# An encoder layer in float32r products: big buffers moved by 32 bytes, four raw weight buffers in the first up product, layer norm in finer pieces, two groups of steps one unit earlier

## The reference

```python
h   = x @ w_in          # recurrent branch, gate, two attentions
y   = concat(rms(rglru(h) * gelu(gate)), rms(band_attention(h)), rms(forgetting_attention(h)))
x   = LN1(alpha * x + y @ w_out)
x   = LN2(alpha * x + relu(x @ w_up) ** 2 @ w_down)
# LN(x) = (x - mean) * rsqrt(var + eps) * g + b
```

## Time and profile before

| | us |
|---|---|
| median of 3 runs (lowest, highest) | 2536.57 (2535.47, 2537.32) |
| the profiled execution | 2535.64 |
| its span, first to last instruction | 2533.7 |
| TensorE busy | 2420.8 |
| VectorE busy | 1291.5 |
| ScalarE busy | 843.5 |

### The profile page before, as it was taken

One profiled execution on the slowest core, in us unless ns is written; L12 is line 12 of the kernel. 1 busy time (PEld: TensorE's weight loads), 2 busy tenths in 40 slices (PEclk: granted clock), 3 DMA queues, 4 the chain that ended last, 5 costly groups with the idle time before them and its releaser, 6 DMA issues.

```text
span 2533.7 us, 41915 instructions
## 1 busy us (share of the span) xinstructions
PE 2420.8 (96%) x17703; PEld 2371.6 (94%) x17703; DVE 1291.5 (51%) x1092; ACT 843.5 (33%) x891; POOL 125.6 (5%) x183
## 2 busy tenths in 40 slices
PE   8999999996996989898999999989999999999997
PEld 7999999995885989898999999989999999999997
DVE  3312555335446577556777777753333333333358
ACT  3222444215333355653444444431212121111132
POOL 2000233100020100000000000000000000000000
PEclk9999999998997999999999999999999999999999
DMA  7222333324441456674555555572323323323244
GB/s 207 83 83 70 104 110 96 102 90 141 127 150 43 150 175 206 203 240 133 170 170 170 170 170 170 170 251 84 120 80 118 112 84 121 122 84 121 84 167 158
DMA packets 310768, 342.43 MB, mean 135 GB/s; under 512 B 11124, under 2 KB 284728, under 8 KB 310088
## 3 DMA queue, kind: packets, MB, share of 16 engines
q1 hardware_dynamic: 271888, 291.95, 36.5%
q10 hardware_dynamic: 35912, 36.49, 4.2%
q0 software_dynamic: 2864, 12.44, 1.5%
HBM read 295.95 MB, written 46.47 MB: 135 GB/s over the span
## 4 chain that ended last, share of the span: by engine, by line
PE 90%; DVE 5%; ACT 2%; issue 2%; DMA 1%; ACTq 0%; DVEq 0%; SPq 0%
PE psum L419 53%; PE psum L1841 29%; PE psum L1949 4%; DVE w_lo L409 1%; PE psum L1795 1%; ACT w_hi L873 1%; PE psum L1709 1%; ACT w_hi L405 0%; PE psum L1750 0%; DVE resid L1118 0%; PE psum L1764 0%; DMA raw<-in_w_up 0%; DVE ln_sumsq L1217 0%; PE psum L1936 0%; PE psum L1653 0%
## 5 line engine op out<-in xcount | busy, mean ns | idle before, releaser
L409 DVE TENSOR_TENSOR w_lo<-raw,w_hi 128x2048 fp32r<-128x2048 f32 x168 | 390.1, 2322 | 493.7 <-ACT w_hi L405 425.1
L405 ACT ACTIVATE w_hi<-raw 128x2048 fp32r<-128x2048 f32 x138 | 264.2, 1915 | 895.7 <-PE psum L419 760.5
L419 PE MATMUL psum<-x_hi,w_hi 128*128 128x288 f32 x1280 | 278.7, 299 | 3.1 <-DVE w_lo L409 3.1
L419 PE MATMUL psum<-x_lo,w_hi 128*128 128x288 f32 x1280 | 275.1, 296 | 0.0
L419 PE MATMUL psum<-x_hi,w_lo 128*128 128x288 f32 x1280 | 275.1, 296 | 0.0
L1841 PE MATMUL psum<-x_b_hi,w_hi 128*128 128x288 f32 x768 | 230.9, 301 | 20.6 <-DVE w_lo L409 11.9
L1430 DVE TENSOR_TENSOR acc<-psum,acc 128x576 f32<-128x576 f32 x96 | 72.7, 757 | 347.3 <-PE psum L419 347.3
L1841 PE MATMUL psum<-x_e_hi,w_hi 128*128 128x288 f32 x768 | 228.2, 297 | 9.8 <-DVE w_lo L1352 9.8
L1841 PE MATMUL psum<-x_b_hi,w_lo 128*128 128x288 f32 x768 | 230.3, 300 | 0.0
L1841 PE MATMUL psum<-x_e_hi,w_lo 128*128 128x288 f32 x768 | 228.7, 298 | 0.0
L419 PE MATMUL psum<-h_hi_even,w_hi 128*128 128x288 f32 x1024 | 220.4, 296 | 6.5 <-DVE h_lo_even L1416 6.5
(11 more groups left out here) (335 smaller groups left out, 4841.6 us busy)
## 6 DMA issues: line engine op xcount, KB each, us to landing
raw<-in_w_down SPq DMA_DIRECT2D x72, 1024.0 KB, 5.3
raw<-in_w_up SPq DMA_DIRECT2D x64, 1024.0 KB, 6.0
raw<-in_w_in SPq DMA_DIRECT2D x40, 1024.0 KB, 5.4
raw<-in_w_out SPq DMA_DIRECT2D x24, 1024.0 KB, 5.3
a_even<-in_w_up SPq DMA_DIRECT2D x24, 1024.0 KB, 6.4
h_scratch<-c_tile ACTq DMA_DIRECT2D x48, 288.0 KB, 2.2
h_even<-h_scratch SPq DMA_DIRECT2D x8, 1152.0 KB, 8.1
h_odd<-h_scratch SPq DMA_DIRECT2D x8, 1152.0 KB, 10.7
```

The costliest lines, as they stand in the source:

```text
L405: act.activation(WH[s][:, :, :], RAW[s][:, :, :], ACT.Copy).then_inc(hi_done, 1)
L409: dve.tensor_tensor(WL[s][:, :, :], RAW[s][:, :, :], WH[s][:, :, :].bitcast(F32), ALU.subtract).then_inc(lo_done, 1)
L419: last_mm = pe.matmul(PS[:, 2 * to + h, 0:c], w, x[:, kk, HALF * h:HALF * h + c], start=(first and n == 0), stop=(final and n == 2))
```

## The change

1. A spare buffer of 32 bytes per partition is put ahead of the large buffers. All of them then start on multiples of 64 bytes. Some small buffers inside (gate weights, `tr`, `a`, `u`, the forget weights) move from multiples of 64 to 32 past one.
2. In 1A, units 0 to 19 use four raw buffers (`RAW`, and two new ones where the lo parts of y rows 8 to 15 lie until w_out is done), units 20 to 31 two.
3. The reductions over 8 tiles are replaced: each square tile is folded by one 128 x 1152 add (`fold`), the two are added (`join`), and TensorE sums the four 288-column pieces with its ones matrix. So `variance` makes 4 float32 matmuls for 2, and `mean(1)` 4 for 2.
4. The layer norm steps are spread: one quarter at a time where two stood together, and for h = 0 the variance is read after unit 11, where it was read in unit 13. F1 and F2 are split one unit earlier. For h = 1, `shifted(1)` and `shifted(3)` go ahead of the snapshot of the next groups. The combinations come two units later.
5. `sigma1` and `sigma2` of the first superblock are made during the last unit of 1A, ahead of its last add.
6. The split of the first chunk of h goes ahead of the last add of phase 1B.

```diff
+N_DEEP = 20
+        sb("align_64_bytes", [128, 8])
...
+            for a in range(2 * N_SB):
+                if a == 2 * N_SB - 2:
...
+                buf, landed, _ = raw_1a(a)
+                if a in (2, 3):
+                    sp.wait_ge(unit_done, N_1A + 2)
+                else:
+                    sp.wait_ge(lo_done, N_1A + a + (1 if a < 2 or a >= N_DEEP + 2 else -1))
+                sp.dma_start(buf[:, :, :], up_unit(0, a % 2, a // 2)).then_inc(landed, 16)
...
+            def hi_1a(a):
+                buf, landed, count = raw_1a(a)
+                act.wait_ge(landed, count)
+                act.wait_ge(unit_done, N_1A + a + 1)
+                act.activation(WH[a % 2][:, :, :], buf[:, :, :], ACT.Copy).then_inc(hi_done, 1)
...
+                elif g in (6, 7):
+                    shifted(2 * (g - 6) + 1, 1)
-                elif g == 8:
+                elif g == 9:
                     act.wait_ge(combo, 1)
                     factor_hi(F5, X1["b00"])
...
+            def fold(T, n, p, h):
+                dve.wait_ge(ln_sq, 2 * h + p + 1)
+                a = T[:, 0:n, :]
+                dve.tensor_tensor(a, a, T[:, n:2 * n, :], ALU.add).then_inc(ln_ss, 1)
+            def join(h):
+                dve.wait_ge(ln_ss, 3 * h + 2)
+                a = SQ[0][:, 0:4, :]
+                dve.tensor_tensor(a, a, SQ[1][:, 0:4, :], ALU.add).then_inc(ln_ss, 1)
...
             for a in range(2 * N_SB):
+                if a == 2 * N_SB - 1:
+                    dve.wait_ge(unit_done, N_1B + 1)
+                    sigma1(0, 0)
+                    sigma2(0, 0)
...
-                for n in range(2):
-                    mm = pe.matmul(PS[:, 5, 0:HALF], ones[:, :], NV[n][:, :], start=(n == 0), stop=(n == 1))
+                for n in range(4):
+                    mm = pe.matmul(PS[:, 5, 0:HALF], ones[:, :], SQ[0][:, n, :], start=(n == 0), stop=(n == 3))
```

More of the change, by code:

```diff
@@ L202, in encoder_step @@
         r = Region()
-        NS = [r.sb(f"ln1_sum{i}", [128, HALF]) for i in range(3)]
-        NV = [r.sb(f"ln1_sumsq{p}", [128, HALF]) for p in range(2)]
+        NS = r.sb("ln1_sum", [128, HALF])
         ND, RS = (r.sb(n, [128, HALF]) for n in ("ln1_sd", "ln1_rstd"))
@@ L208, in encoder_step @@
         F7, F3 = ([r.sb(f"x1_{n}_{p}", [128, UK, HALF], F32R) for p in ("hi", "lo")] for n in ("e7", "b11"))
+        r.close()
+        r = Region()
+        r.sb("y_lo_upper", [128, UK * TOK])
+        RAWX = [r.sb(f"raw_extra{s}", [128, UK, UC]) for s in range(2)]
         r.close()
@@ L269, in encoder_step @@
         raw_in = [sem(f"raw_in{s}") for s in range(2)]
+        rawx_in = [sem(f"raw_extra_in{s}") for s in range(2)]
         hi_done, lo_done = sem("hi_done"), sem("lo_done")
@@ L936, in superblock @@
                 act.dma_start(h_rows(0, g)[:, :, HALF:TOK], CQ[0][:, :, :]).then_inc(c_out[0], 16)
+                if end:
+                    for p in range(4):
+                        h_split(0, 0, p)
                 if not end:
@@ L1352, in lo_1b, with lo_1a @@
                 dve.tensor_tensor(WL[par][:, :, :], src[:, :, :], WH[par][:, :, :].bitcast(F32), ALU.subtract).then_inc(lo_done, 1)
+            def lo_1a(a):
+                buf, _, _ = raw_1a(a)
+                dve.wait_ge(hi_done, N_1A + a + 2)
+                dve.tensor_tensor(WL[a % 2][:, :, :], buf[:, :, :], WH[a % 2][:, :, :].bitcast(F32), ALU.subtract).then_inc(lo_done, 1)
+            for v in range(16):
+                add_out(v, 0)
+                if v == 8:
+                    for m in range(2):
+                        dve.wait_ge(o_ev[m], 8)
+                    centre(0, 0)
+                elif v == 9:
+                    centre(3, 0)
+                elif v == 12:
+                    rstd(0)
+                    scaled(0, 0)
+                elif v == 13:
+                    scaled(3, 0)
+                add_out(v, 1)
+                if v == 8:
+                    centre(1, 0)
+                elif v == 10:
+                    fold(SQ[1], 4, 1, 0)
+                elif v == 12:
+                    scaled(1, 0)
+                n = N_O2 + v + 2
+                if v < 14:
+                    lo(dve, n // 2, n % 2)
+                else:
+                    lo_1a(v - 14)
+                if v == 8:
+                    centre(2, 0)
+                elif v == 9:
+                    fold(SQ[0], 4, 0, 0)
+                elif v == 10:
+                    join(0)
+                elif v == 12:
+                    scaled(2, 0)
+                elif v == 13:
+                    factor_lo(F1, X1["b00"], 1)
+                elif v == 14:
+                    factor_lo(F2, X1["b10"], 2)
@@ L1387, in superblock @@
                     lo(dve, G_D, 0)
+                    for p in range(4):
+                        h_remainder(0, 0, p)
                 dve.wait_ge(unit_done, unit_1b(g, 4) + 3)
@@ L1395, in superblock @@
                     lo(dve, G_D, 1)
-            dve.wait_ge(unit_done, N_1B + 1)
-            sigma1(0, 0)
-            sigma2(0, 0)
             dve.wait_ge(sig, 2)
```

241 lines of the change are left out of this document (106 added, 135 removed).

## The result

| | before | after |
|---|---|---|
| median, us (lowest, highest) | 2536.95 (2535.47, 2539.39) | 2520.16 (2518.71, 2521.33) |
| profiled execution, its span | 2535.64, 2533.7 | 2520.07, 2518.3 |

These medians are of four executions each. The ratio is 0.9933, 95% interval 0.9921 to 0.9946: faster by 0.67%. The forecast was 2520.7. That the number is met does not make every term of the sum right, so the gain is first divided by stage. The starts are those of TensorE's first matmul in each stage, read from the timelines of the two profiled executions.

The account below looks back on a forecast made before the run. TensorE, busy 96% of the span, bounds the kernel, so only its work and waits count. Gains less costs sum to 15.9 us off the profiled 2535.64: 2519.7, plus 0.93 for the median, 2520.7; range 2400 to 2542.

Parts of the forecast that it names:

- I am wrong if the pace moved: Closing test: forecast wrong if the matmul pace moved, or if ScalarE waits for raw buffers anywhere in 1A.
- 32 bytes: Large buffers moved to multiples of 64 bytes: no effect on VectorE, DMA or TensorE, taken as 0.
- Start of 1A: Phase 1A's first matmul: 4.7 us earlier, at about 925.4, wait left 2.7, plus 1.0 for less slow clock.
- Finer norm, units 13 and 14: Norm in 1A: gains 2.1 and 2.7 us at unit 13; costs 2.0 for rows, 2.4 and 1.0 at unit 14.
- Four raw buffers: Raw-buffer loads in 1A: one visible ScalarE wait, costing at most 0.9 us, removed; gain 0.9.
- Sigma: Wait before the first sigma unit: 9.8 us down to 3.0, gain 6.8, plus 1.2 for slow clock.
- h: Wait before the down product, 6.5 us: gain 1.9, VectorE's last add of 1B releasing it instead of the remainder.
- Rival 1: All matmuls reach the better token half's pace or just below: 27 us at most, 20 taken, 2501; chance 0.12.
- Rival 3: Weights and moving operand both on multiples of 64 slow every matmul: 2548 at 1.6 ns each; chance 0.08.
- Rival 2: TensorE's fixed 13.3 ns per matmul shrinks: gain of up to about 11 ns, pace 126 or 122; chance 0.30.
- Rival 4: Moved steps in 1A gain nothing: three places with new or lasting waits eat 14 us, 2535; chance 0.07.
- The half-counted slow stretches: Behind shortened waits, half the 1.2 GHz slow stretch credited: 1.0 at 1A's start, 1.2 at sigma.

Follow-up runs that it names:

- no_pad: The changed kernel without the spare buffer of 32 bytes, all else as changed; 2521.45 us, ratio to before 0.9944.
- again: The changed kernel itself run once more, unaltered; 2520.35 us (2512.26 to 2521.49), ratio to before 0.9925.
- pad_alone: The kernel before with only the 32 spare bytes added; 2533.92 us, ratio to before 0.9989.
- norm_back: The changed kernel with scalings and shifts of h = 1 in pairs again, the adds kept; 2520.56 us, ratio to before 0.9932.
- two_raw: The changed kernel with two raw buffers throughout phase 1A; 2518.36 us, ratio to before 0.9934.
- sigma_back: The changed kernel with the two first sigma sums behind the last add of 1A again; 2525.40 us, ratio to before 0.9957.
- h_back: The changed kernel with the first h chunk's splits and remainders behind all of 1B again; 2523.46 us, ratio to before 0.9944.
- better: The changed kernel with 1B's last add behind the first h remainder and h = 1 shifts one place later; 2507.21 us, ratio to before 0.9877.

## Why the forecast was right, and where only its sum was
The moved steps are best tested by `no_pad`, which has them without the bytes. Its stages against those of before gained 5.4 us (1A starts at 924.72), 7.3 (1A took 227.48), 2.4 (1B took 517.87) and -1.0 (the down product), 14.1 in all, against 4.7, 8.1, 3.1 and 0, 15.9 in all. So the mechanism was right for the steps that carry the gain (the start of 1A, sigma, h), and the sum of all steps was 1.8 us too high, less than the clock alone moves 1A from one execution to the next. That the forecast of the changed kernel came within 0.5 us is in part luck, as the terms below show. By the prediction's own test, "I am wrong if the pace moved", it was wrong on the 32 bytes.

- **Start of 1A**: forecast 925.4, measured 923.24. The chain was right, the wait 3.0 for 2.7. Without the bytes it is 924.72, so 0.7 us of the difference are the steps, and the rest comes with the bytes, by w_in's faster pace (1.5 us here, 3.2 in `again` with 921.56), which the term "32 bytes: 0" did not have. This step, the largest but sigma, was not taken back by itself: its 5.4 us are read from the wait, 8.4 before and 3.0 in `no_pad` and in the changed kernel, 8.6 in `pad_alone`.
- **Finer norm, units 13 and 14**: chain and distance right to 0.1 us (8.86 for 8.8). The two gains and two costs of this part sum to 1.4; `norm_back` measured none that stands out of the clock's scatter. The cost of 2.0 for the added float32 rows was not tested by a run of its own. That the slow stretch "goes, or is swallowed by the next wait" held in one execution and not in the other.
- **Four raw buffers**: 0.9 forecast, 0 measured (`two_raw`). The term was an upper bound ("at most 0.9"), taken as the value. The wait of 4.3 us belonged to the old order.
- **Sigma**: 6.8 forecast, 6.7 in the wait, 6.5 in the start of 1B and 5.1 in the median (`sigma_back`). The 1.2 for the clock did not come in the first pair of profiles: 23 slow matmuls for 21.
- **h**: 1.9 forecast, 2.0 measured in the wait (`h_back`), with the releaser named in advance. The same reasoning showed that only the order of one add was in the way, and `better` took it away.
- **32 bytes**: 0 forecast. This is the term that was mis-sized: a gain of 2.9 us in w_in, a loss of 1.2 to 2.2 in 1B (517.87 us in `no_pad`; 519.05 and 520.07 in two executions of the changed kernel), a loss of about 1.5 in 1A (1536 matmuls by 1.0 ns), and by chance a gain of up to 8 in the down product. The parts nearly cancel, and that is luck: nothing in the prediction said that they would. Rival 1 (all at the better pace) came true as far as some stretches go: 130.0 ns is even below the 131.8 that I had as the better half, and with 96 bytes it is 10 us of gain. Rival 3 (every matmul slower) came true in 1A and 1B of the changed kernel alone, by about 1 ns. The slowest place, 64 spare bytes, 5.8 us above `again`, has the large buffers 32 past a multiple of 64 and the weights on one, so the rival's mechanism, both on a multiple of 64, is not what makes it slow.
- **Rival 2** (the 13.3 ns are the price of a bad start) is refuted at four places out of four: no stretch fell below 130.0 ns. The Trainium skill, "TensorE: Matmul & The Clock Gate", section "Back-to-back issue gap", has a formula for matmuls issued singly that would have given 122.5 ns for 288 columns; no stretch of these runs comes near it. I gave this rival 0.30, too much for a mechanism whose only support was a number that a fixed cost explains as well; the lower end of the range, 2400, came from it alone.
- **Rival 4** (no gain from the moved steps) fell with `no_pad`, 2521.45 for the 2535 that it gave.
- **The half-counted slow stretches**, 1.0 at the start of 1A and 1.2 at sigma, were both too high: a wait of 3 us brings the low clock as one of 8 or 10 does. Over all profiles some 10 to 24 slow matmuls stand behind the 23 waits of 3.0 to 3.1 us at these two places, about 15 on average, and 15 to 23 behind the five of 8.4 to 9.8 us, about 19 on average: 0.4 us apiece. The whole stretch was gained only where the wait fell to 0.85 us or went.

## What to carry to other kernels
Read which operation ends a wait, and ask what stands queued ahead of it that nobody is waiting for: one 0.75 us add behind three remainders cost 3.6 us of wait and 1.9 of slow clock. Credit a shorter wait with little more than its own length; the clock came back in full only where a wait fell from 4.5 to 0.85 us or went. Where matmuls run back to back for most of the time, try the place of the large buffers in steps of 32 bytes for itself, with several executions of each: it was worth 16 us between the worst and the best here, as much as the reordering, and no profile of one place shows it.

## What the hardware showed that I had not expected
- The pace of a 288-column float32r matmul averages 130.0, 131.8, 132.2 to 132.4 or 133.3 ns over a stretch at full clock, set by stage and by where the large buffers start; it repeats from execution to execution except for the next point. The Trainium skill, "SBUF — State Buffer", section "Specifications (TRN2)", has lines of 16 bytes, from which I had taken that a shift of 32 changes nothing; for TensorE these runs disagree with that. For VectorE nothing changed: the lo halves took 2283 ns after, 2284 before. Which operand meets what in the memory was not settled. Only the buffers behind the spare one were moved, all together and with the small ones among them, while the weights stayed; to move single operands is an open experiment.
- With 32 spare bytes the down product has a second pace, 130.0 ns. In all three profiles that have it, it begins with TensorE's first matmul behind a wait (of 6.4, 4.5 and 1.24 us) and holds for exactly one piece; the two that are followed by a break are slower again behind it. A piece of 2304 matmuls gains 7.3 us. So the pace changed only where TensorE stood still or the matmuls changed. What decides it was not found.
- In the profiled executions, from the start of 1A to the end of the down product, the clock fell to 1.2 GHz behind every wait of 3.0 us or more, for 10 to 24 matmuls, and the length of the wait tells little about that number. It fell behind some waits of 2.0 to 2.3 us and not behind others, and not behind those of 2.5 and 2.7 (`before`, `pad_alone`). Of the waits from 0.7 to 1.82 us it fell behind a single one, that of 1.82 in the down product of `two_raw`.
